# Attention of the first token chunk: from the q,k,v stage to the stage of the gates

## The chip, the cores and the metric

One Trainium2 chip with 8 cores. The kernel runs on all 8, each core on one sequence of the batch (4096 tokens of 1024 channels), with no exchange between them. The metric is the device time in microseconds (us) of the slowest core, median of the runs. A core has five engines that run side by side, each in its own program order: TensorE (PE) for matmuls, VectorE (DVE), ScalarE (ACT), GpSimd (POOL) and SyncE (SP), which here issues most DMAs.

## What is computed

One decoder layer: an attention mixer and a recurrent mixer in parallel, merged by gates, then a squared-ReLU MLP. Cut to what matters here:

```python
h = rmsnorm(x, norm1_w[l])
z = h @ w_in[l]
q, k, v, xr, yr, ga, gr = jnp.split(z, split_points, axis=-1)
...
o_attn = moba_attention(qh, kh, vh, rel_bias)     # 256-blocks: own causal block + top 3 past blocks
...
hr = rg_lru(causal_depthwise_conv(xr, ...), ...)
o_rnn = hr * jax.nn.gelu(yr)
g_attn = jax.nn.sigmoid(ga + b_gate[l, 0])
g_rnn = jax.nn.sigmoid(gr + b_gate[l, 1])
merged = g_attn * (o_attn @ w_proj_attn[l]) + g_rnn * (o_rnn @ w_proj_rnn[l])
x = x + merged @ w_out[l]
h2 = rmsnorm(x, norm2_w[l])
x = x + jnp.square(jax.nn.relu(h2 @ w_ff1[l])) @ w_ff2[l]
```

A query looks at its own block and at most three past blocks, so the first chunk of 512 tokens (blocks 0 and 1), and the second (blocks 2 and 3) leave no past block out.

## The kernel before

The sequence is cut into 32 token tiles of 128 (`NT`) and 8 chunks of 512 (`NCH`). The program is written as a list of operations with what each reads and writes; a planner (`Prog.schedule`) with a cost for each kind of operation then sets the order on every engine, greedily by readiness, and `keep_busy` puts matmuls on a tile of ones (`fill`, tile `onesf`, 128x512, the only matmuls recorded under line L1412) wherever its plan shows TensorE idle for over 0.7 us. They write nothing that is read. All other operations are recorded under L530, DMAs under L535, so rows are told apart by tile names.

Three stages follow one another on TensorE.

*q,k,v stage* (0 to about 262 us): for each token tile the norm and transposes (`FEn`), q and k with their norm (`FEp`), v (`FEv`). From tile 10 on, units of `attention0()` stand among them: attention of chunk 0 from tiles that never leave the chip (`qc0`, `kc0`, `vc0`), one unit per head and key tile: a score matmul on 64 rows ("S"), the bias on DVE, exp on ACT into `PTa`, and up to four 65-column matmuls with v ("AV"). The bias table `BT` is made for that at tiles 5 to 9, by way of a gather (`hk2`) on the POOL queue. The result goes to DRAM (`oT_s`).

*Stage of the gates* (to about 829 us), `stageB(s, g)`: x and y projections and the recurrence of chunk s (`RNN`, `RNN2`), the attention gate of chunk s (`GA`, weights `wga`), and the recurrence gate and projection of chunk s-1 (`GR`, weights `wgr`, `wpr`). For chunk 0, `GA` also multiplies by `P_attn` (weights `wps`) and `GR` adds both halves, so that the merged `mT` of chunk 0 goes to DRAM (`mT_s`). Other chunks store the two halves apart (`t1_s`, `rm_s`).

*Attention and MLP* (to the end): two lists are merged. The dense list holds the last eight units of `GR`, then for each chunk W1, W2, W1 of the second half with `gating(c+1)` between (loads of the two halves into `t1r`, `rmr`, matmul with `wpa`), `outproj(c+1)` and W2. The attention list holds `attention(c)` for c from 1. `outproj(0)` stands ahead of both lists, on the `mT` loaded by `early()`. In `attention(c)` a unit's S matmul has 64 rows for c = 1 and 80 for c > 1: the 16 more carry the block mask (`qT` rows 64 to 79, written by `GM`, against the block pattern `cE_d`). S uses two PSUM banks, and three after the last `GR`.

SP, ACT, DVE and PE wait in order: an instruction whose operand isn't ready holds all behind it on its engine, an issue on SP too.

Of the kernel before, what the change touches and what calls it, by code (L numbers as in the profile page):

```python
# [20 lines left out]
NEG = -30000.0  # L21
# [389 lines left out]
def build_nc():  # L411
# [37 lines left out]
    oT_s = scr("oT_s", [128, 4, CH], BF16)  # L449
    mT_s = scr("mT_s", [128, 8, CH], BF16)  # L450
# [28 lines left out]
    with root:  # L479
# [95 lines left out]
        wrow = alloc("wrow", [384], F32)
        Js = alloc("Js", [128], BF16)
        hk2 = alloc("hk2", [NH, 256], BF16)
        endA0 = cur[0]
        st.pop().close()
        cur[0] = endX  # L580
# [3 lines left out]
        assert endA0 <= endR  # L584
# [18 lines left out]
        qst = [alloc("qstr%d" % i, [4, 256], BF16) for i in range(2)]  # L603
        kst = [alloc("kstr%d" % i, [4, 256], BF16) for i in range(2)]
        vst = alloc("vst", [NH, VW], BF16)
# [5 lines left out]
        hT = [alloc("hT%d" % i, [8, 128], BF16) for i in range(NHT)]  # L611
        pA_peak = cur[0]
# [22 lines left out]
        for v_, vk in ((vc0, "vc0"), (vst, "vst")):  # L635
            op("gpsimd", "memset", [], [vk], ap=v_.rearrange("p a b -> p (a b)"), constant=1.0)

        def bias_table(late):
            op("vector", "memset", [], ["tabx"], ap=tabx[32:33, :], constant=NEG)
            dma("sync", tabx[0:32, :], relb_d, "c1a", [], ["tabx"], extra=late)  # L640
            dma("sync", Gs[0:33, :], cG_d, "c1b", [], ["Gs"], extra=late)
            dma("sync", Js, cJ_d, "c1c", [], ["Js"], extra=late)

        def bias_table1():
            b = tbank()
            op("tensor", "matmul", ["tabx", "Gs"], ["B%d" % b], out=bankf[b][0:8, 0:384], lhsT=tabx[0:33, :], rhs=Gs[0:33, :], start=True, stop=True)
            op("vector", "tensor_copy", ["B%d" % b], ["wrow"], out=wrow[0:8, :], in_=bankf[b][0:8, 0:384])
            dma("sync", scr_w, wrow[0:8, :], "c2", ["wrow"], ["scr_w"])
            dma("gpsimd", hk2, bass.AP(scr_w.tensor, 0, [[1, 128], [384, NH], [1, 256]]), "c3", ["scr_w"], ["hk2"])

        def bias_table2(g):
            b = rbank()
            op("tensor", "matmul", ["hk2", "Js"], ["B%d" % b], out=bankf[b], lhsT=Js, rhs=hk2[:, 2 * g:2 * g + 2, :].rearrange("p a b -> p (a b)"), start=True, stop=True)
            op("vector", "tensor_copy", ["B%d" % b], ["BT"], out=BT[:, 2 * g:2 * g + 2, :], in_=bankf[b].rearrange("p (a b) -> p a b", a=2, b=256))
# [45 lines left out]
        def FEv(t):  # L700
            c, tl = t // TPC, t % TPC
            v_, vk = (vc0, "vc0") if c == 0 else (vst, "vst")
            b = FEmm(t, 2)
            op("scalar", "copy", ["B%d" % b], [vk], out=v_[:, :, 0:260].rearrange("p h (t e) -> p h t e", t=4)[:, :, tl, 0:64],
               in_=bankf[b].rearrange("p (a b) -> p a b", a=8, b=64))
            if tl == TPC - 1:
                dma("sync", v_s[:, c], v_, vk, [vk], ["v_s%d" % c])

        def FEp(t, j):
# [20 lines left out]
            if c == 0:  # L730
                qk_, kk_, o_ = "qc0:%d" % t, "kc0:%d" % t, t * 128
                q_, k_ = qc0, kc0
            else:
                qk_, kk_ = "qstr%d" % g, "kstr%d" % g
                q_, k_ = qst[g], kst[g]
            if j == 0:
                op("vector", "tensor_copy", ["B%d" % b], [qk_], out=q_[:, :, o_:o_ + 128], in_=src)
                if t % 2 == 1 and c > 0:
                    dma("sync", q_s[c, nb_ % 2], q_, qk_, [qk_], ["q_s%d_%d" % (c, nb_ % 2)])
                return  # L740
            op("scalar", "activation", ["B%d" % b, "qkw"], [kk_], out=k_[:, :, o_:o_ + 128], in_=src, func=AF.Identity, scale=qkw)
# [737 lines left out]
```

How the kernel before makes its waits and increments, by code:

```python
        def run(ename, h):  # L335
            for i in order[ename]:
                for s, v in waits[i]:
                    h.wait_ge(sems[s], v)
                ins = ops[i].fn(h)
                if sig[i] is not None:
                    ins.then_inc(sems[sig[i][0]], 16 if ops[i].dsem is not None else 1)
            if ename == "sync":
                for s, v in fw.items():
                    h.wait_ge(sems[s], v)
```

## Time and profile before

| | |
|---|---|
| median of 3 runs | 2318.37 us (2316.98 to 2527.23) |
| the profiled execution | 2318.37 us, span of its slowest core 2316.8 us |
| other cores | 2306.9 to 2316.8 us |
| busy: PE, ACT, DVE, POOL | 2270.7, 1325.2, 1166.7, 621.5 us |
| fills on ones | 126 in the program |

The profiled execution has the median's time; 1.6 us lie outside the span. A row of the order in time gives the start, the duration and the instructions merged. Matmuls overlap, and their ends are modelled, so what one costs is read from the starts of neighbours, not from its duration. "idle before" in brackets is the wait, and what ended it.

### The profile page before, as it was taken

To read this page: it belongs to the slowest core of one execution; us is meant where nothing else is said; L and a number is where in the kernel's file an instruction comes from. 1 tells how busy PE (TensorE), PEld (TensorE's weight loads), DVE (VectorE), ACT (ScalarE), POOL (GpSimd) and SP (SyncE) were. 2 spreads that over 40 slices of the span, in tenths; PEclk is the share of its full clock that TensorE was granted. 3 is DMA by queue.
4 is the path that set the end of the run, shared out by engine and by line. 5 is a ranking of instruction groups with operands and counts; after the bars stand their busy time and mean duration, and the time that the engine had idled before them with its cause. 6 is when DMAs were issued, how large, how long until landed. Compare 5 with 4: busy or idle time off the path is not lost.

```text
span 2316.8 us, 43869 instructions; the slowest of 8 cores (2306.9 to 2316.8 us)
## 1 busy us (share of the span) xinstructions
PE 2270.7 (98%) x14604; PEld 1107.7 (48%) x14604; DVE 1166.7 (50%) x2185; ACT 1325.2 (57%) x2343; POOL 621.5 (27%) x602
## 2 busy tenths in 40 slices
PE   7999999999999999999999999999999999999999
PEld 3445444444444444454545555554555555554444
DVE  4688588787877864454253343324323422233322
ACT  4666576667676755475646646654656465562111
POOL 5776545443444430010011011102001100111200
PEclk9999999999999999999999999999999999999999
DMA  8976734676763365475455565546656554544543
GB/s 194 271 196 176 156 94 113 128 132 142 128 136 83 127 176 169 137 212 176 149 186 163 161 195 161 168 145 180 187 150 175 173 159 159 184 148 141 172 160 127
DMA packets 191559, 370.11 MB, mean 160 GB/s; under 512 B 14819, under 2 KB 105740, under 8 KB 173324
## 3 DMA queue, kind: packets, MB, share of 16 engines
q1 hardware_dynamic: 183532, 331.65, 45.9%
q0 software_dynamic: 7808, 35.65, 11.7%
q8 instruction: 124, 2.03, 0.4%
q14 instruction: 95, 0.78, 0.1%
HBM read 331.32 MB, written 90.71 MB: 182 GB/s over the span
## 4 chain that ended last, share of the span: by engine, by line
PE 89%; DMA 4%; issue 3%; DVE 2%; ACT 1%; POOL 1%; SPq 1%; DVEq 0%; ACTq 0%; POOLq 0%
PE bank L530 89%; DMA s_t1r<-t_s 1%; DMA s_nw<-nw_bc 1%; DMA s_hk<-scr_w 1%; POOL s_ssq L530 1%; SPq L535 1%; DMA s_wga<-wr_p 0%; DMA t_s<-s_t 0%; DMA s_qT<-s_mskT 0%; DVE s_cv L530 0%; DMA s_Vr<-v_s 0%; PE bank L1412 0%; ACT s_junk L530 0%; DVE s_ii L530 0%; DVE s_t1r L530 0%
## 5 line engine op out<-in xcount | busy, mean ns | idle before, releaser
L530 ACT ACTIVATE s_PT<-bank 128x512 bf16<-128x512 f32 (+1 forms) x1120 | 578.7, 566 | 319.1 <-PE bank L530 226.8
L530 PE MATMUL bank<-s_h2T,s_wsl 128*128 128x512 bf16 x2048 | 523.3, 379 | 0.0
L530 PE MATMUL bank<-s_uT,s_wsl 128*128 128x512 bf16 x2048 | 511.3, 379 | 0.0
L530 PEld LDWEIGHTS bank<-s_Vr,s_PT 128*128 128x128 bf16 x4144 | 262.9, 97 | 244.0 <-issue 12.8
L530 PE MATMUL bank<-s_qT,s_kTr 80*128 80x512 bf16 (+2 forms) x1120 | 361.6, 364 | 2.3 <-DMA s_qT<-s_mskT 2.3
L530 ACT ACTIVATE s_rl<-bank 128x512 f32<-128x512 f32 x256 | 152.7, 597 | 266.3 <-PE bank L530 254.9
L530 PE MATMUL bank<-s_Vr,s_PT 128*128 128x65 bf16 x4144 | 299.5, 193 | 3.9 <-ACT s_PT L530 2.3
L530 PEld LDWEIGHTS bank<-s_h2T,s_wsl 128*128 128x128 bf16 x2048 | 189.3, 98 | 180.5 <-issue 7.6
L530 PEld LDWEIGHTS bank<-s_uT,s_wsl 128*128 128x128 bf16 x2048 | 185.1, 98 | 171.5 <-issue 3.9
L530 POOL TENSOR_TENSOR s_uT<-s_rl 128x512 bf16<-128x512 f32 x80 | 83.8, 1048 | 620.1 <-ACT s_rl L530 617.6
L530 DVE TENSOR_TENSOR s_uT<-s_rl 128x512 bf16<-128x512 f32 x176 | 123.5, 702 | 248.1 <-ACT s_rl L530 247.7
L530 DVE TENSOR_TENSOR s_x1T<-bank,s_x1T 128x512 f32<-128x512 f32 x128 | 88.3, 690 | 315.8 <-PE bank L530 315.5
L530 DVE TENSOR_TENSOR bank<-bank,s_BT 128x256 f32<-128x256 f32 (+1 forms) x312 | 111.8, 377 | 161.7 <-PE bank L530 160.1
L530 PE MATMUL bank<-s_wqkv,s_hT 128*128 128x512 bf16 x768 | 184.5, 381 | 0.4 <-ACT s_hT L530 0.2
L530 DVE SCALAR_TENSOR_TENSOR s_cv<-s_xr,s_pvec,s_cv 128x512 f32<-128x512 f32 x192 | 163.4, 917 | 1.4 <-issue 0.6
L530 POOL TENSOR_TENSOR s_orn<-s_ii,s_gq 128x512 bf16<-128x512 f32 x64 | 115.7, 1820 | 116.5 <-DVE s_ii L530 116.4
L530 POOL TENSOR_TENSOR s_ss<-s_ss,s_sqt 128x512 f32<-128x512 f32 x48 | 60.9, 1269 | 284.9 <-ACT s_sqt L530 283.8
L530 PE MATMUL bank<-s_mT,s_wo 128*128 128x512 bf16 x512 | 132.9, 379 | 4.2 <-DVE s_mT L530 2.7
L530 POOL TENSOR_TENSOR s_mT<-s_t1r,s_rmr 128x512 bf16<-128x512 f32 x28 | 36.8, 1315 | 352.3 <-DVE s_t1r L530 250.8
L530 PEld LDWEIGHTS bank<-s_qT,s_kTr 80*128 80x128 bf16 (+1 forms) x1120 | 104.3, 98 | 50.2 <-issue 10.4
L530 PE MATMUL bank<-s_hTb,s_wga 128*128 128x512 bf16 x512 | 123.1, 383 | 3.1 <-DMA s_wga<-wr_p 3.1
L530 ACT ACTIVATE s_t<-bank,s_hbias 128x512 f32<-128x512 f32 x128 | 82.8, 680 | 71.1 <-PE bank L530 68.6
(137 smaller groups left out, 2854.5 us busy)
## 6 DMA issues: line engine op xcount, KB each, us to landing
s_wsl<-wff_s SPq DMA_DIRECT2D x128, 1024.0 KB, 5.8
s_xs<-x SPq DMA_DIRECT2D x32, 512.0 KB, 8.4
t_s<-s_t SPq DMA_DIRECT2D x64, 256.0 KB, 6.8
wff_s<-wff_p POOLq DMA_DIRECT2D x16, 1024.0 KB, 16.2
s_x1T<-xT SPq DMA_DIRECT2D x64, 256.0 KB, 3.8
outT<-s_x1T SPq DMA_DIRECT2D x64, 256.0 KB, 5.6
s_t1r<-t_s SPq DMA_DIRECT2D x56, 256.0 KB, 4.0
rm_s<-s_t SPq DMA_DIRECT2D x56, 256.0 KB, 5.7
```

The costliest lines, as they stand in the source:

```text
L530: return P.add(eng, lambda e, m=meth, kw=kw: getattr(e, m)(**kw), reads, writes, cost=c_, lat=lat, fam=fam, tag=tag or (writes[0] if write ...
L535: return P.add(q, lambda e: e.dma_start(out=out, in_=in_), reads, writes, dsem=dsem, cost=(1000.0 if q == "gpsimd" else 80.0), nbytes=nb, ...
```

## The change

`attention0()`, the merge of chunk 0 within `GA` and `GR` and the DRAM copies `oT_s`, `mT_s` are gone. Chunk 0 is now treated as the others: its q, k, v go to DRAM by `qst`, `kst`, `vst`; `attention(0)` runs in the last stage, ahead of `attention(1)`; then come `gating(0)` and `outproj(0)` at the end of the first dense stretch, ahead of W1 of chunk 0. Its S matmuls, and those of chunk 1, have 80 rows, with mask. The bias table is made later: its first matmul at tile 14, the gather behind the gate weights on the POOL queue, the rest in `stageB(2, 0)`. SBUF addresses of the last two stages are laid out anew; `wga`, `wgr`, `wpr` now alternate, panel by panel. Of what the words of the change name, the matmuls on constants (`keep_busy`) and the order of the `wqkv` loads are in both kernels alike.

```diff
-            if t == 9:
-                for g in range(4):
-                    bias_table2(g)
-                at0 = attention0()
-            if t >= 10:
-                for _ in range(2 if t < 24 else 4):
-                    if at0:
-                        at0.pop(0)()
...
-            if c == 0:
-                b = bank()
-                for kt in range(4):
-                    op("tensor", "matmul", ["oTb", "wps%d" % (p % 2)], ["B%d" % b], tag="pa", ...
...
-                op("tensor", "matmul", ["orn%d" % sos[kt], "wpr%d" % p], ["B%d" % b], tag="pr", ...
+                op("tensor", "matmul", ["orn%d" % i for i in sos] + ["wpr%d" % p], ["B%d" % b], tag="pr", ...
...
-            if c == 0:
-                dma("sync", t1x[s], t1_s[0, m], "t1x%d" % s, ["t1_s0_%d" % m], ["t1x%d" % s])
-                op("gpsimd", "tensor_tensor", ["t2_%d" % s, "t1x%d" % s], ["mst%d" % s], ...
...
-            if b >= 4:
+            if b >= 3:
...
-                        qk = ["qT%d:%d0" % (s, h % 2), "qT%d:%d1" % (s, h % 2)]
-                        kr = 64
-                        if c > 1:
-                            qk += ["qT%d:m%d" % (s, h), "kTr%d:E" % ks]
-                            kr = 80
...
+                           lhsT=kTr[ks][0:80, ...], rhs=qT[s][0:80, h, q0:CH], start=True, stop=True)
...
         def early():
+            dma("sync", wpa, wpo[:, 0:4, :], "wpa", ["wpo_s0"], ["wpa"])
             for i in range(2):
-                dma("sync", mT[:, 4 * i:4 * i + 4, :], mT_s[:, 4 * i:4 * i + 4, :], ...
                 dma("sync", wo[:, 4 * i:4 * i + 4, :], wpo[:, 4 + 4 * i:8 + 4 * i, :], ...
+            for _, f in at0[0:5]:
+                f()
+            first.append(kv0(0, 0))
 
         stageB(NCH - 1, 1, early)
-        for _, f in outproj(0):
-            f()
-        at1.pop(0)[1]()
-        first.append(kv1(1, 0))
...
+        g0 = gating(0)
         for m in range(8):
             extend([(3460.0, gate1u(m))])
+            if m == 5:
+                marks[0] = len(dense)
+            if m > 5:
+                extend(g0[2 * m - 12:2 * m - 10])
+        extend(g0[4:5])
+        for i in range(3):
+            dense.append((0.0, WLOAD))
+            extend(g0[5 + i:6 + i])
+        extend(outproj(0))
+        dense.append((6000.0, lambda: None))
```

The order that the planner makes of it. First PE where the q,k,v stage meets the gates (numbers are buffers; `cvb` against `wbda`, `wbdi` belongs to the recurrence), before:

```order
L530 MATMUL bank4<-s_cvb0,s_wbda 128x512
L530 MATMUL bank5<-s_cvb0,s_wbdi 128x512
L530 MATMUL bank1<-s_oTb,s_wps0 128x512 x4
L530 MATMUL bank6<-s_cvb1,s_wbda 128x512
L1412 MATMUL bank0<-s_onesf 128x512 x2
L530 MATMUL bank7<-s_identb,s_ktm1 128x128 x4
L530 MATMUL bank3<-s_oTb,s_wps0 128x512 x4
L1412 MATMUL bank0<-s_onesf 128x512 x6
L530 MATMUL bank0<-s_hTb0,s_wga0 128x512 x8
```

and now PE in the same place, from the first matmul with `wga`:

```order
L528 MATMUL bank2<-s_hTb0,s_wga1 128x512 x4
L528 MATMUL bank7<-s_identb,s_ktm1 128x128 x4
L528 MATMUL bank3<-s_cvb0,s_wbdi 128x512
L528 MATMUL bank2<-s_hTb0,s_wga1 128x512 x4
L528 MATMUL bank4<-s_hTb0,s_wx2 128x512 x3
L528 MATMUL bank7<-s_cvb2,s_wbdi 128x512
L528 MATMUL bank4<-s_hTb0,s_wx2 128x512 x2
L528 MATMUL bank3<-s_hTb0,s_wga1 128x512 x8
L528 MATMUL bank4<-s_hTb0,s_wx2 128x512 x3
L528 MATMUL bank5<-s_hTb0,s_wy2 128x512 x5
L528 MATMUL bank0<-s_hTb0,s_wga0 128x512 x8
```

Panel 1 of `wga` comes ahead of panel 0, projections stand between, and the fills are gone. Next PE behind the last gate matmuls of the stage of the gates (`qT,kTr` are S, `Vr,PT` AV, `mT,wo` is `outproj`), before:

```order
L530 MATMUL bank<-s_hTb,s_wgr 128x512 x4
L530 MATMUL bank<-s_mT,s_wo 128x512 x32
L530 MATMUL bank<-s_hTb,s_wgr 128x512 x4
L1412 MATMUL bank<-s_onesf 128x512 x9
L530 MATMUL bank<-s_hTb,s_wgr 128x512 x8
L1412 MATMUL bank<-s_onesf 128x512 x9
L530 MATMUL bank<-s_mT,s_wo 128x512 x32
L530 MATMUL bank<-s_orn,s_wpr 128x512 x8
```

and now, in the same place:

```order
L528 MATMUL bank<-s_qT,s_kTr 128x384
L528 MATMUL bank<-s_qT,s_kTr 128x512
L528 MATMUL bank<-s_hTb,s_wgr 128x512 x14
L1318 MATMUL bank<-s_onesf 128x512 x9
L528 MATMUL bank<-s_hTb,s_wgr 128x512 x16
L1318 MATMUL bank<-s_onesf 128x512 x14
L528 MATMUL bank<-s_orn,s_wpr 128x512 x5
L528 MATMUL bank<-s_Vr,s_PT 128x65 x4
L528 MATMUL bank<-s_qT,s_kTr 128x256
```

The 64 `outproj` matmuls no longer stand there; 96 fills in 25 places lie between the last gates of this stage and W1, where there were 20 in 3. Last SP in the same place (`rm_s` are the stores of `GR`), before:

```order
L535 DMA s_qT<-q_s 64x4x256 x4
L535 DMA s_Vr<-v_s 128x2x288 x4
L535 DMA rm_s<-s_t_0 128x512
L535 DMA rm_s<-s_t_1 128x512
L535 DMA rm_s<-s_t_0 128x512
```

and now SP there, from the last store of chunk 6:

```order
L533 DMA rm_s<-s_t_1 128x512
L533 DMA s_qp<-q_s 128x4x256 x2
L533 DMA s_Vr<-v_s 128x2x288 x4
L533 DMA s_qT<-q_s 64x4x256 x4
L533 DMA s_kTr<-c_E 16x4096
L533 DMA s_kTr<-k_s 64x4x256 x4
L533 DMA s_t1r<-t_s 128x512
L533 DMA rm_s<-s_t_0 128x512
L533 DMA rm_s<-s_t_1 128x512
```

Fifteen loads of chunk 1 and one of `gating(0)` stand ahead of the next stores of `GR`; further on, `gating(0)` adds eight pairs of loads.

## Rows read from the trace of the kernel before

**Rows 1.** The page, busy time of TensorE.
```profile
PE 2270.7 (98%) x14604; PEld 1107.7 (48%) x14604; DVE 1166.7 (50%) x2185; ACT 1325.2 (57%) x2343; POOL 621.5 (27%) x602
```

**Rows 2.** The page, chain that ended last, by engine.
```profile
PE 89%; DMA 4%; issue 3%; DVE 2%; ACT 1%; POOL 1%; SPq 1%; DVEq 0%; ACTq 0%; POOLq 0%
```

**Rows 3.** Windows: length, busy PE, PEld, DVE, ACT, POOL; then granted clock, DMA share, GB/s.
```profile
36.00:128.00 92.00, 86.07 (x543) 43.54 (x544) 64.77 (x104) 58.44 (x97) 68.36 (x88) 1.00 0.92 245
128.00:262.00 134.00, 132.60 (x866) 68.56 (x865) 105.72 (x197) 86.09 (x153) 89.09 (x109) 1.00 0.63 171
262.00:275.00 13.00, 8.30 (x45) 3.71 (x44) 4.81 (x9) 7.67 (x11) 7.23 (x10) 1.00 0.98 187
275.00:280.00 5.00, 5.00 (x17) 1.92 (x16) 0.69 (x1) 0.69 (x1) 3.31 (x4) 0.66 1.04 190
280.00:345.00 65.00, 62.68 (x288) 27.55 (x286) 55.87 (x79) 49.01 (x76) 31.30 (x25) 1.00 0.44 105
829.00:885.00 56.00, 52.65 (x260) 23.14 (x258) 30.84 (x49) 24.41 (x38) 15.53 (x11) 1.00 0.54 141
```

**Rows 4.** PE in order of time, chunk 1, S of 64 rows.
```profile
859.36 0.28 PE L530 MATMUL bank<-s_Vr,s_PT 128*128 128x65 bf16 x4 [1.24 <-DMA s_Vr<-v_s]
859.58 0.39 PE L530 MATMUL bank<-s_qT,s_kTr 64*128 64x512 bf16 x1
859.89 0.39 PE L530 MATMUL bank<-s_orn,s_wpr 128*128 128x512 bf16 x1
```

**Rows 5.** PE in order of time, a later chunk, S of 80 rows.
```profile
1117.62 0.28 PE L530 MATMUL bank<-s_Vr,s_PT 128*128 128x65 bf16 x4
1117.74 0.38 PE L530 MATMUL bank<-s_qT,s_kTr 80*128 80x512 bf16 x1
1117.96 1.68 PE L530 MATMUL bank<-s_h2T,s_wsl 128*128 128x512 bf16 x7
```

**Rows 6.** PE in order of time, first fills behind 36 us.
```profile
92.63 1.67 PE L1412 MATMUL bank<-s_onesf 128*128 128x512 bf16 x7
```

**Rows 7.** PE in order of time, where the stage of the gates begins.
```profile
274.72 5.30 PE L530 MATMUL bank<-s_hTb,s_wga 128*128 128x512 bf16 x16 [3.07 <-DMA s_wga<-wr_p]
...
282.66 3.62 PE L530 MATMUL bank<-s_hTb,s_wga 128*128 128x512 bf16 x16
```

**Rows 8.** PE in order of time, from that stage's end to W1.
```profile
837.82 2.11 PE L1412 MATMUL bank<-s_onesf 128*128 128x512 bf16 x9
840.25 1.89 PE L530 MATMUL bank<-s_hTb,s_wgr 128*128 128x512 bf16 x8 [0.32 <-ACT s_t L530]
841.97 2.11 PE L1412 MATMUL bank<-s_onesf 128*128 128x512 bf16 x9
845.55 7.07 PE L530 MATMUL bank<-s_mT,s_wo 128*128 128x512 bf16 x32 [1.48 <-DVE s_x1T L530]
...
888.23 0.59 PE L1412 MATMUL bank<-s_onesf 128*128 128x512 bf16 x2
888.66 2.75 PE L530 MATMUL bank<-s_h2T,s_wsl 128*128 128x512 bf16 x12
```

**Rows 9.** POOL in order of time, last results of the recurrence.
```profile
843.41 3.34 POOL L530 TENSOR_TENSOR s_orn<-s_ii,s_gq 128x512 bf16<-128x512 f32 x2 [3.09 <-DVE s_ii L530]
```

**Rows 10.** SP in order of time, the same place.
```profile
850.08 2.53 SPq L535 DMA_DIRECT2D s_qT<-q_s  x4
...
856.69 16.59 SPq L535 DMA_DIRECT2D rm_s<-s_t  x5
```

**Rows 11.** DMA issues: KB each, median us to landing.
```profile
s_t1r<-t_s SPq DMA_DIRECT2D x56, 256.0 KB, 4.0
```

**Rows 12.** Chain in order of time, a wait for such a load.
```profile
1192.74 8.46 DMA s_t1r<-t_s
```

**Rows 13.** Groups by shape: busy, mean ns of one, idle before.
```profile
L530 DVE SCALAR_TENSOR_TENSOR s_t1r<-s_t1r,bank 128x512 f32<-128x512 f32 x56 | 38.3, 684 | 36.1 <-PE bank L530 25.4 <-DMA s_t1r<-t_s 10.1
L530 POOL TENSOR_TENSOR s_mT<-s_t1r,s_rmr 128x512 bf16<-128x512 f32 x28 | 36.8, 1315 | 352.3 <-DVE s_t1r L530 250.8 <-DVE bank L530 47.5 <-DVE s_rcp L530 46.0
```

More of the change, by code:

```diff
@@ L634, in build_nc @@
         op("vector", "memset", [], ["hstate"], ap=hstate, constant=0.0)
[L635 to L636 removed]
+        for i in range(1):
+            op("gpsimd", "memset", [], ["vst%d" % i], ap=vst[i].rearrange("p a b -> p (a b)"), constant=1.0)
         def bias_table(late):
[L639 to L642, printed above, removed]
+            op("vector", "memset", [], ["ii0"], ap=tabx[32:33, :], constant=NEG)
+            dma("sync", tabx[0:32, :], relb_d, "c1a", [], ["ii0"], extra=late)
+            dma("sync", Gs[0:33, :], cG_d, "c1b", [], ["cv0"], extra=late)
@@ L651, in bias_table2 @@
[L651 to L654, printed above, removed]
+            op("tensor", "matmul", ["ii0", "cv0"], ["B7"], out=bankf[7][0:8, 0:384], lhsT=tabx[0:33, :], rhs=Gs[0:33, :], start=True, stop=True)
@@ new lines, in bias_table1, with bias_table2, bias_table3 @@
+            op("vector", "tensor_copy", ["B7"], ["rr0"], out=wrow[0:8, :], in_=bankf[7][0:8, 0:384])
+            dma("sync", scr_w, wrow[0:8, :], "c2", ["rr0"], ["scr_w"])
+        def bias_table2():
+            dma("sync", Js, cJ_d, "c1c", [], ["Js"])
+            dma("gpsimd", hk2, bass.AP(scr_w.tensor, 0, [[1, 128], [384, NH], [1, 256]]), "c3", ["scr_w"], ["hk2"])
+        def bias_table3():
+            for g in range(4):
+                b = dbank()
+                op("tensor", "matmul", ["hk2", "Js"], ["B%d" % b], out=bankf[b], lhsT=Js, rhs=hk2[:, 2 * g:2 * g + 2, :].rearrange("p a b -> p (a b)"), start=True, stop=True)
+                op("vector", "tensor_copy", ["B%d" % b], ["BT"], out=BT[:, 2 * g:2 * g + 2, :], in_=bankf[b].rearrange("p (a b) -> p a b", a=2, b=256))
@@ L1059, in build_nc @@
[L1059 to L1068 removed]
+        t1r = [alloc("t1r0", [CH], F32)]
@@ new lines, in build_nc @@
+        assert cur[0] <= endR, (cur[0], endR)
+        if endR - cur[0] > 64:
+            alloc("gap2", [(endR - cur[0]) // 64 * 32], BF16)
+        mT = alloc("mT", [8, CH], BF16)
+        oT.append(alloc("oT1", [4, CH], BF16))
+        NRL = 2
+        rl = [alloc("rl%d" % i, [CH], F32) for i in range(NRL)]
+        t1r.append(alloc("t1r1", [CH], F32))
+        rmr = [alloc("rmr%d" % i, [CH], F32) for i in range(2)]
+        assert cur[0] <= baseC, (cur[0], baseC)
+        uT = alloc("uT", [16, CH], BF16)
@@ L1069, in build_nc @@
+        NW = 4
+        wsl = [alloc("wsl%d" % i, [4096], BF16) for i in range(NW)]
+        NX1 = 12
+        x1T = alloc("x1T", [NX1, CH], F32)
+        h2T = alloc("h2T", [8, CH], BF16)
         p2_peak = cur[0]
@@ L1207, in attention @@
             units.append((0.0, lambda: QLOAD(c)))
-            if c > 1:
-                units += [(100.0, lambda tl=tl: GM(c, tl)) for tl in range(TPC)]
+            units += [(100.0, lambda tl=tl: GM(c, tl)) for tl in range(TPC)]
             for h in range(NH):
@@ L1233, in WLOAD @@
             s = i % NW
-            dma("sync", wsl[s], wff_s[i % 16], "wsl%d" % s, ["wff_s%d" % (i % 16)], ["wsl%d" % s])
+            dma("sync", wsl[s], wff_s[i % 16], "wsl%d" % s, ["wff_s%d" % (i % 16)], ["wsl%d" % s], extra=P.after("mT:%d" % i) if i < 3 else ())
         def gating(c):
@@ L1387, in build_nc @@
                 extend(w2)
-        queue = [(u[0], u[1], 1) for u in at1]
-        for c in range(2, NCH):
-            for u in attention(c):
+        queue = [(u[0], u[1], 0) for u in at0[5:]]
+        tot0 = sum(q_[0] for q_ in queue)
+        for c in range(1, NCH):
+            us = attention(c)
+            if c == 1:
+                queue[16:16] = [(u[0], u[1], 0) for u in us[:5]]
+                us = us[5:]
+            for u in us:
                 queue.append((u[0], u[1], c))
```

223 lines of the change are left out of this document (59 added, 164 removed).

## Prediction

> **What bounds the kernel now.** I read the page first. TensorE is busy 98% of the span [rows 1], and the chain that ended last lies on it for 89% [rows 2]: what counts is the matmul time in program order, and the places where TensorE waits. No other engine comes near. So every part of the change is priced on TensorE: work that vanishes or appears there, fills that do, and pauses.
>
> A busy share hides what a matmul costs, since a matmul's row overlaps the next one's. The order in time gives the cost, from start to start. Eight 512-column matmuls take 841.97 - 840.25 = 1.72 us [rows 8], so 0.215 us for one, a fill too. Then I looked for pauses by stage, as length minus busy time [rows 3]: 5.9 us from 36 to 128, 1.4 to 262, 4.7 in the 13 us where the gates begin, 2.3 from 280 to 345, and 3.4 from 829 to 885, where the last stage begins.
>
> **The change part by part.** The attention of chunk 0, its gating matmuls (32 with `wpa` for 32 with `wps`) and its output projection exist on both sides. Moved work that meets a TensorE without idle time costs the same there. What is left is six terms.
>
> *Scores on 80 rows instead of 64: -17.7 us.* In chunk 1 an AV of four takes 859.58 - 859.36 = 0.22 us and the S behind it 859.89 - 859.58 = 0.31 [rows 4]. In a later chunk, with 80 rows, they take 0.12 and 0.22 [rows 5]. The columns are the same, so each stretch of 64-row matmuls costs 0.19 us more, about half going in and half coming out. Chunk 0 and chunk 1 have 96 such S, which stand in 93 separate stretches of the order; 93 x 0.19 = 17.7. All of them stand beside dense matmuls, so TensorE pays it today, and no cover is lost with it. The Trainium skill speaks on both sides here. "TensorE: Matmul & The Clock Gate", section "Why this matters for your kernels", has a single matmul on few rows take as long as one on 128, which leaves nothing to save, and the sum would be 17.7 us higher. "TensorEngine Tiling (Array Packing)", section "Key Properties", says that changing the tiling mode drains the engine, which would be this term, without a price. The two rows agree with the second.
>
> *Fills that go from the first two stages: -5.4 us.* From 36 to 345 us there were 27 in 7 places (the first: [rows 6]); 2 are left. 25 x 0.215 = 5.4. Fills run whether or not TensorE would have waited, so this is sure.
>
> *Pauses in the first two stages: -6 us, between -2 and -11.* They are 14.3 us from 36 to 345 [rows 3]. The wait of 3.07 us for the first `wga` panel [rows 7] should go, and what else TensorE waits in those 13 us, 4.7 in all: the loads of `wps` ahead of the panel are gone, and the order puts `wga1` ahead of `wga0`, with projections between. The rest comes from norms and recurrence, which stay. The bias gather moves behind the gate weights on POOL, and nobody waits for it until the third chunk.
>
> *The clock behind that wait: -1.7 us.* The 16 `wga` matmuls after it take 5.30 us, the same 16 later 3.62 [rows 7], and the granted clock from 275 to 280 is 0.66 [rows 3], so partly the lower of its two levels, after a stretch of waits. If the wait goes, so do these 1.7 us.
>
> *Fills in the last stage: +17.4 us.* Between the end of the gates and W1 there are 96 instead of 20, and behind that 23 instead of 18: 81 x 0.215 = 17.4, as sure as the fills above. They mark where the planner found nothing to do. Before, `outproj(0)` filled the time until the recurrence of chunk 7 is done: its last results land at 843.41 + 3.34 = 846.75 [rows 9], 17.7 us after the last gate groups of that stage at 829. Now only 32 gate matmuls (6.9 us) and two S (0.4) can run there, so some 10.4 us are open, 23 fills (4.9 us) among them. After that the attention of chunk 0 is paced by S, bias, exp, AV on two score banks; the gate matmuls run out before its heads do.
>
> *Pauses that the fills don't cover: +15 us, between -2 and +39.* Behind the two groups of nine, which themselves take 1.94 us, 0.49 and 1.64 us were lost [rows 8]; behind the group of two at 888.23 the next starts 0.43 later, so nothing. The mean of three is 0.7; 25 places give 17.5, less the 2.1 of today, which is 15. The lower end is no pause at all, the upper one 1.64 at each place. I take the mean, since the nearest rows are in the same stage; the 5.5 us still open above are part of it.
>
> *Loads on SP: +7 us, between 0 and +21.* One issue of a q load takes 2.53 / 4 = 0.63 us [rows 10]. The 15 loads of chunk 1 ahead of the stores of `GR` hold SP for some 9 us, and with it the two buffers `t2` and the banks behind them. Today 18 issues stand there too, and the stores come at 856.69 [rows 10], but `outproj(0)` covers it; now the heads of chunk 0 do, in part: I take 4, between 0 and 9. Further on, `gating(0)` has two buffers for eight pairs of loads, so three rounds follow the first, each a load, a DVE product of 0.68 and a POOL sum of 1.3 us [rows 13]. At the median landing of 4.0 us [rows 11] with 0.3 of issue a round is 6.3 us and three are 19; beside them TensorE has the 64 units of chunk 1, where a full unit is 0.34 us [rows 5], so at most 22 us, in fact about 18 since a quarter of them are cut, and some 14 fills, 3 us. That just covers it. At 8.46 us, as in the chain later [rows 12], three rounds are 32, and 12 stick out. I take 3. What queues behind on SP are the loads of x for `outproj(0)` and of the W1 slabs; TensorE waits for both.
>
> *Small:* 16 more mask and gate matmuls, each shorter than a fill; under 1 us, I take 0.7.
>
> The sum: -17.7 - 5.4 - 6 - 1.7 + 17.4 + 15 + 7 + 0.7 = +9.3 us, on the profiled execution's 2318.37, which is also the median: 2328 us. With all favourable ends it is -17.7 - 5.4 - 11 - 1.7 + 17.4 - 2 + 0 + 0.7 = -19.7, so 2299; with all unfavourable ones -17.7 - 5.4 - 2 - 0 + 17.4 + 39 + 21 + 0.7 = +53, so 2371.
>
> **The rivals.** *The chain of chunk 0 becomes the path (slower).* Place: attention 0, `gating(0)`, `outproj(0)`, norm, W1, one behind the other, beside whatever GR and chunk 1 still have. It decides from a landing of `t1r` of about 4.7 us, where three rounds outlast the 21 us beside them; at 8.46 us and with 1.64 us lost in front of each of the 25 places, the result is the upper end, 2371. For it: TensorE's order is fixed, so one late load holds all behind it, and the sixteen loads of `gating(0)` come one round after the other. Against it: the planner that set the order knew these dependencies, and before, its pauses came out small [rows 8].
>
> *The waits don't appear (slightly faster).* The fills run, but behind them the operands are there: no pauses and no stall on SP, 2318.4 - 30.8 + 17.4 - 2 + 0.7 = 2304. For it: the third group of today lost nothing. Against it: the 10.4 us behind the recurrence are open whatever the fills do [rows 9].
>
> *The 64 rows were not the cause.* If the extra 0.19 us came with the place and not with the rows, or if a single short matmul costs as much as a full one (the rule in "TensorE: Matmul & The Clock Gate" above), the first term falls away: 2346. The two pairs of rows speak against it.
>
> That the change doesn't do what its words say holds in part: fills and the order of the `wqkv` loads are in both kernels. It has no time of its own, since the sum uses only what differs.
>
> **How the numbers follow.** My forecast, a small loss from terms that nearly cancel, gets 0.62; the slower rival 0.16, the faster one 0.15, the 64 rows 0.05; 0.02 are left for a gain that I don't see. A measurement of this kernel can tell about 2%, 46 us, from no change. The forecast, the faster rival and the third lie within that. The slower rival ends above 2365, and most of its chance counts as slower, some more from the forecast's tail: 0.17. Faster by over 2% needs 46 us, while all savings together are 36: 0.03. The range, 2302 to 2366, leaves about 0.15 above and 0.05 below.
>
> **What would show it.** All S have 80 rows, AV takes 0.12 and S 0.22 in chunks 0 and 1 too. The first two stages end some 30 us sooner (attention and `wps` out of them, and the terms above), around 798; W1 begins around 912, where it was 885, and from there the stages run alike, shorter by what chunk 1 had left. No wait for `wga0`, and a clock of 1.00 there. Between the gates and W1 some 96 fills and 15 to 25 us of pauses. Wrong I would be if the pauses there were over 40 us, if a wait of several us dropped the clock there as at 275, or if the later stages, which I take as unchanged, waited on loads that now come in another order.

## The result and the profile after

The changed kernel takes 2379.84 us (median of 4 runs, 2372.06 to 2384.7), the kernel before 2317.74 beside it: a ratio of 1.0266, interval 1.0225 to 1.0307. It is slower by some 62 us; 9 were forecast, with 2366 as the upper end of the range. Some executions of all these kernels were disturbed, and the ratios compare the others, so the text goes by ratios; in us they are the ratio times 2318.4.

The page of the profile after first, with the lines that answer to [rows 1, 2]; the line PEclk gives the granted clock in 40 slices of the span:

```profile
span 2374.1 us, 44166 instructions; the slowest of 8 cores (2339.4 to 2374.1 us)
PE 2292.8 (97%) x14676; PEld 1116.1 (47%) x14676; DVE 1170.3 (49%) x2225; ACT 1328.0 (56%) x2343; POOL 613.8 (26%) x593
PE   7999789999999988999999999999999999999999
PEclk9999999999999997999999999999999999999999
PE 83%; DMA 5%; issue 4%; DVE 3%; POOL 3%; ACT 1%; SPq 1%; DVEq 0%; POOLq 0%; ACTq 0%
```

A busy share of 97% instead of 98% looks harmless. The slices say where to look: the fifth and the sixth (237 to 356 us), and the 15th and 16th (831 to 950 us), in the second of which the clock drops too. The chain lies on PE for 83% instead of 89% [rows 2].

The same in windows of the changed kernel (length, PE busy, number of instructions, granted clock, DMA share, GB/s), to set against [rows 3]:

```profile
36.00:128.00 92.00, 85.95 (x544) 1.00 0.85 248
...
262.00:275.00 13.00, 6.12 (x29) 0.93 0.69 146
275.00:280.00 5.00, 0.62 (x2) 0.50 0.61 107
...
400.00:450.00 50.00, 44.51 (x200) 0.97 0.60 114
...
825.00:912.00 87.00, 75.57 (x468) 0.96 0.54 154
912.00:945.00 33.00, 28.02 (x182) 0.60 0.86 253
945.00:965.00 20.00, 18.15 (x104) 0.98 0.07 19
```

Where the gates begin, 11 of 18 us are empty. Just before W1 TensorE is busy, but at a granted clock of 0.60, so for most of it on the lower of its two levels. Apart from a load at the very start (14.97 us), the three longest transfers on the chain, in order of time, stand at these places:

```profile
251.04 22.25 DMA q_s<-s_qst
...
429.42 17.36 DMA rm_s<-s_t
...
907.43 13.96 DMA s_t1r<-t_s
```

All three carry 256 KB; the load that I took from [rows 11] lands in 4.0 us. The first was the dearest. POOL in order of time (in brackets: idle before, and what ended it):

```profile
254.04 0.53 POOL L533 DMA_DIRECT2D s_wgr<-wr_p  x1 [0.41 <-PE bank L528]
257.34 1.03 POOL L528 TENSOR_TENSOR s_rr<-s_aa 128x512 f32<-128x512 f32 x1 [2.78 <-DVE s_aa L528]
273.88 0.57 POOL L533 DMA_DIRECT2D s_wpr<-wpr_p  x1 [15.51 <-DMA q_s<-s_qst]
274.48 2.04 POOL L528 TENSOR_TENSOR s_rr<-s_aa 128x512 f32<-128x512 f32 x2
```

and PE:

```profile
267.09 1.03 PE L528 MATMUL bank<-s_hTb,s_wy 128*128 128x512 bf16 x4
279.38 0.59 PE L528 MATMUL bank<-s_cvb,s_wbda 128*128 128x512 bf16 x1 [11.27 <-ACT s_t L528]
```

and ACT, which stands between the two:

```profile
275.62 0.63 ACT L528 ACTIVATE s_rr<-s_rr 128x512 f32<-128x512 f32 x1 [14.57 <-POOL s_rr L528]
...
278.55 1.27 ACT L528 ACTIVATE s_t<-bank,s_hbias 128x512 f32<-128x512 f32 x2
```

The fourth `wpr` panel takes the place in SBUF where the last q tile is staged, so its load, on POOL, waits for that tile's store. Behind it in POOL's queue stand the squares of the recurrence (`rr`). ScalarE waits 14.57 us for these, its `s_t` behind them frees no bank, and TensorE stands still for 11.27 us. Who was in the store's way is seen in the DMA issues from 240 to 262 us (queue 0 is POOL's, queue 1 SP's; packets, MB, share of the engines; then KB and us to landing):

```profile
q0 software_dynamic: 1133, 2.19, 69.3%
q1 hardware_dynamic: 1065, 2.27, 34.2%
...
s_hTb<-h_s SPq DMA_DIRECT2D x1, 1024.0 KB, 21.3
s_wga<-wr_p POOLq DMA_DIRECT2D x2, 512.0 KB, 13.5
s_wgr<-wr_p POOLq DMA_DIRECT2D x2, 512.0 KB, 19.3
v_s<-s_vst SPq DMA_DIRECT2D x1, 576.0 KB, 23.0
...
q_s<-s_qst SPq DMA_DIRECT2D x1, 256.0 KB, 22.2
```

On its own queue the store follows a load of 1 MB and a store of 576 KB, and POOL's gate panels take as many bytes as that whole queue. On core 1 the load of `hTb` lands in 7.1 us (issued at 241.70; until 248.8 SP's queue moves 1.23 MB and POOL's 0.18), the q store in 9.8, and TensorE loses 3.2 us there, not 11. Cores 1, 3 and 7 are of this kind, the five others of the first.

For all cores, medians over the eight of each run, from the first and last matmul of the groups with `wga`, `h2T` (W1) and `uT` (W2); the range is that of the cores:

| kernel | last wga, us | from there to W1 | W1 to the last W2 |
|---|---|---|---|
| before | 822.9 (819.6 to 828.3) | 59.8 | 1423.6 |
| after | 818.6 (803.4 to 824.7) | 135.0 | 1400.0 |
| forecast, as a change | -31 | +58 | -18 |
| measured, as a change | -4 | +75 | -24 |

The profiled core of after, 4, is the worst: last `wga` at 824.7, then 140.7 us, then 1404.0. Against the profiled core of before (825.5, 60.0, 1427.0) that is -0.8, +80.7 and -23.0, together the 57 us between the spans.

### The profile page after: what moved, and what is told of

It reads as the page before. It is cut to its first block, busy times and chain, and to the rows that moved or that the text cites. A ratio compares the mean times of both kernels' runs of the same rounds, so it can differ in the third digit from the quotient of the medians.

```text
span 2374.1 us, 44166 instructions; the slowest of 8 cores (2339.4 to 2374.1 us)
## 1 busy us (share of the span) xinstructions
PE 2292.8 (97%) x14676; PEld 1116.1 (47%) x14676; DVE 1170.3 (49%) x2225; ACT 1328.0 (56%) x2343; POOL 613.8 (26%) x593
## 4 chain that ended last, share of the span: by engine, by line
PE 83%; DMA 5%; issue 4%; DVE 3%; POOL 3%; ACT 1%; SPq 1%; DVEq 0%; POOLq 0%; ACTq 0%
PE bank L528 82%; POOL s_ssq L528 2%; DMA s_t1r<-t_s 1%; DMA q_s<-s_qst 1%; SPq L533 1%; DMA rm_s<-s_t 1%; DMA s_nw<-nw_bc 1%; DVE s_cv L528 1%; DMA outT<-s_x1T 1%; PE bank L1318 1%; DVE s_ii L528 0%; DMA s_qT<-s_mskT 0%; DVE s_ssq L528 0%; DMA s_x1T<-xT 0%; DVE s_t1r L528 0%
## 5 line engine op out<-in xcount | busy, mean ns | idle before, releaser
L528 ACT ACTIVATE s_PT<-bank 128x512 bf16<-128x512 f32 (+3 forms) x1152 | 590.1, 563 | 314.0 <-PE bank L528 192.1
L528 PE MATMUL bank<-s_uT,s_wsl 128*128 128x512 bf16 x2048 | 518.9, 379 | 1.7 <-DVE s_x1T L528 1.0
L528 PE MATMUL bank<-s_h2T,s_wsl 128*128 128x512 bf16 x2048 | 516.8, 380 | 0.8 <-DVE s_h2T L528 0.8
L528 PEld LDWEIGHTS bank<-s_Vr,s_PT 128*128 128x128 bf16 x4224 | 272.8, 98 | 262.7 <-issue 26.6
L528 PE MATMUL bank<-s_qT,s_kTr 80*128 80x512 bf16 (+3 forms) x1152 | 373.0, 367 | 6.3 <-DMA s_qT<-s_mskT 3.1
L528 PE MATMUL bank<-s_Vr,s_PT 128*128 128x65 bf16 x4224 | 314.1, 194 | 5.5 <-ACT s_PT L528 4.8
L528 PEld LDWEIGHTS bank<-s_qT,s_kTr 80*128 80x128 bf16 x1152 | 108.3, 99 | 51.1 <-issue 12.6
L528 PE MATMUL bank<-s_orn,s_wpr 128*128 128x512 bf16 x512 | 124.6, 385 | 5.0 <-POOL s_orn L528 5.0
```

The source lines that it names most:

```text
L528: return P.add(eng, lambda e, m=meth, kw=kw: getattr(e, m)(**kw), reads, writes, cost=c_, lat=lat, fam=fam, tag=tag or (writes[0] if write ...
```

## Experiments

**The theory.** Transfers of 256 KB that share the DMA engines with loads of 0.5 and 1 MB come 10 to 20 us late. TensorE's order is fixed, so what waits for them (a queue, two buffers, a matmul) holds all the rest, and behind such waits the clock falls. **The rival.** No transfer is to blame: the loss is the 17 us of fills and the pace of the last stage (attention 0, one gating round behind the other), which the prediction's slower rival has. Two terms of the prediction, the rows and the fills, are tested beside them.

The measured places of all runs, as in the table above. The median core is the median of the eight spans, as a mean over the executions that the ratio compares (of before, ten from the runs beside late_panels, before_no_fills and before_rows128):

| kernel | ratio to before, interval | median core, us | last wga | to W1 | W1 to end |
|---|---|---|---|---|---|
| before | | 2312.2 | 822.9 | 59.8 | 1423.6 |
| after | 1.0266, 1.0225 to 1.0307 | 2359.1 | 818.6 | 135.0 | 1400.0 |
| late_wpr3 | 1.0175, 1.0155 to 1.0195 | 2354.4 | 811.3 | 139.2 | 1398.3 |
| late_panels | 1.0197, 1.0172 to 1.0221 | 2355.4 | 815.0 | 136.1 | 1399.9 |
| late_slabs | 1.0172, 1.0123 to 1.0222 | 2347.4 | 819.6 | 126.0 | 1402.6 |
| both_late | 1.0136, 1.0121 to 1.0150 | 2342.4 | 809.0 | 126.1 | 1403.9 |
| all_late | 1.0156, 1.0140 to 1.0171 | 2347.1 | 811.2 | 129.0 | 1403.2 |
| no_fills | 1.0273, 1.0178 to 1.0367 | 2370.1 | 826.8 | 142.8 | 1401.9 |
| more_fills | 1.0223, 1.0202 to 1.0245 | 2362.6 | 821.8 | 141.5 | 1396.5 |
| rows_64 | 1.0296, 1.0253 to 1.0339 | 2375.6 | 821.3 | 148.0 | 1401.2 |
| before_no_fills | 1.0024, 1.0014 to 1.0033 | 2317.0 | 826.2 | 60.4 | 1427.2 |
| before_rows80 | 0.9950, 0.9932 to 0.9968 | 2298.2 | 824.7 | 58.3 | 1411.2 |
| before_rows128 | 0.9929, 0.9910 to 0.9948 | 2296.0 | 821.3 | 58.4 | 1411.7 |

The time is the slowest core's, and which cores meet the long store changes from run to run; the median core and the column "to W1" are steadier. From before to after the median core loses 47 us, the slowest 62: the 15 between are that lottery.

**The load behind the store, moved.**

```diff
-            dma("gpsimd", wpr[p], ...)
+            if p < 3:
+                dma("gpsimd", wpr[p], ...)
...
+                if (s, g) == (0, 1):
+                    dma("gpsimd", wpr[3], ..., extra=P.after("orn3"))
```

> The changed kernel with one load moved: the fourth wpr panel is issued on POOL after the first four recurrences of chunk 0, not between the first and the second square of their gates. In the changed kernel that load waits on POOL 15.5 us for the store of the last q tile, which took 22.3 us beside five gate panels of 512 KB each, and TensorE loses 11.3 us behind it. Transfer theory (short transfers that share the DMA engines with bulk loads come 10 to 17 us late, and a queue or a buffer hands that on to TensorE): that wait is gone on all cores that have it, the last wga matmul comes at some 805 to 812 us instead of 818 to 825, and the time falls by 8 to 13 us, to 2367 to 2372. Pace theory (the loss is fills and attention work that the last stage's chain paces; the store is no cause): the wait comes back at the next step of the recurrence, and the time stays at 2376 to 2384.

Measured: 1.0175, 2359 us, 21 us less than after, more than expected. No core has the wait: idle time of TensorE from 252 to 345 us is 8.1 to 10.6 us on all eight, where it was 19.6 to 22.1 on five cores and 9.2 to 10.2 on three. The last `wga` of core 4:

```profile
L528 PE MATMUL bank<-s_hTb,s_wga x512: 376/379/631, 252.5 to 812.1; 128*128 128x512 bf16 x171
```

12.6 us sooner than in after (824.7). The store itself stays slow (21.2 us on that core, 19 to 23 on six of the eight); only nobody waits for it. Most of the gain is the slowest core's: it stood 19 us above the median core in the profiled execution of after and stands 4 above it here. The median core gains 5, since the stretch to W1 has grown from 135.0 to 139.2 us; what takes these 4 us back was not tried.

**The traffic before the store, moved.**

```diff
-  ... "wga%d" % p, [], ["wga%d" % p])
+  ... "wga%d" % p, [], ["wga%d" % p], extra=P.after("q_s7_1") if p == 3 else ())
-  ... "wgr%d" % p, [], ["wgr%d" % p])
+  ... "wgr%d" % p, [], ["wgr%d" % p], extra=P.after("q_s7_1") if p in (0, 3) else ())
```

> The changed kernel in which three gate panels (wga3, wgr0, wgr3) are issued once the store of the last q tile has landed; the fourth wpr panel still waits on POOL for that store, with three gate squares behind it. What changes is the traffic that the store meets: two panels instead of five. Transfer theory: the store lands in 5 to 11 us on all cores instead of 20 to 23 on five of them, POOL's wait shrinks to under 5 us, TensorE's wait of 10 to 12 us there to under 4, the last wga matmul comes at 802 to 814 us, and the time is 2360 to 2372. If the 22 us are the store's own (many small pieces, HBM), not the panels' traffic: store, waits and time stay, 2376 to 2384.

Measured: 1.0197, 2364 us. The wait stays in POOL's queue, but it is short. On core 4 the 1 MB load ahead of the store lands in 7.1 us instead of 21.3. DMA issues and POOL in order of time there:

```profile
s_hTb<-h_s SPq DMA_DIRECT2D x1, 1024.0 KB, 7.1
```

```profile
264.39 0.63 POOL L533 DMA_DIRECT2D s_wga<-wr_p  x1 [2.21 <-DMA q_s<-s_qst]
```

On all eight cores the q stores land in 7.9 to 11.6 us (three of these are medians of two stores) and POOL waits 2.2 to 6.1; TensorE's longest wait there is 2.7. The 1 MB load still takes 14.8 to 16.8 us on four of the cores, so the store need not wait for it to land early. The last `wga` comes at 808 to 820 us, somewhat later than expected. So the 22 us were the panels' traffic, not the store's own. This and the run before settle the first place.

**The slabs, moved.**

```diff
-        for i in range(3):
-            dense.append((0.0, WLOAD))
-            extend(g0[5 + i:6 + i])
+        extend(g0[5:8])
+        for i in range(3):
+            dense.append((0.0, WLOAD))
...
-  extra=P.after("mT:%d" % i) if i < 3 else ())
+  extra=P.after("mT:7") if i < 3 else ())
```

> The changed kernel with the first three weight slabs (1 MB each) loaded after the last mT of chunk 0 instead of after the first, second and third. In the changed kernel the load of the third t1r takes 13.96 us behind two slabs and eight x loads, TensorE loses 0.9 and 2.0 us there, and the granted clock is 0.61 from 912 to 940 us. Transfer theory: the t1r loads land in 4 to 8 us, the clock stays near 1.00 in that stretch or falls for less time, W1 begins 8 to 18 us sooner, and the time falls to 2362 to 2372. Pace theory: the units of chunk 1 are paced by bias and exp whatever the loads do; W1 begins within 4 us of before and the time is 2374 to 2384. If the slabs now come too late for W1, the time is up to 2392 and TensorE waits for the slab at the start of W1.

Measured: 1.0172, 2358 us; from the gates to W1 126.0 us instead of 135.0. The late load on the chain of core 4, and the stretch in which the clock was 0.60:

```profile
902.01 8.29 DMA s_t1r<-t_s
```

```profile
912.00:945.00 33.00, 30.71 (x207) 0.87 0.55 175
```

8.29 us instead of 13.96, and a clock of 0.87; from 800 us to W1 it is 0.93 to 0.98 on the eight cores, where it was 0.90 to 0.95. The time came out a little better than expected, the median core gains 12 us, and on core 4 the mechanism is the theory's. On other cores the longest `t1r` load on the chain goes either way (core 6: 11.72 us in after, 5.23 here; core 1: 8.08 and 10.97), so for them it isn't shown. The edit also changed the planner's order: 88 instead of 96 scores stand ahead of W1, some 2.7 us at 0.34 a unit [rows 5], and W1 to the end is 2.6 us longer. So by the places about 6 of the 9 us are gained, and the rest is moved.

**Both moves.** Both edits together.

> The changed kernel with both moves together: the fourth wpr panel behind the first recurrences, the three slabs behind the last mT of chunk 0. Alone they gave 2360 and 2362, after 2380. Transfer theory: they act at different places, so they add up: the last wga at some 810 us, W1 some 125 us later, 2338 to 2348. If one only uncovers what the other hides, the time is 2352 to 2362.

Measured: 1.0136, 2350 us, just above the expected 2338 to 2348. On the median core they do add up, 5 and 12 to 17 us, and by place: last `wga` at 809, then 126.1 us. The order of late_slabs is in it, with 88 scores ahead of W1. What does not add up is the slowest core's part, which each move alone had gained in some measure.

**The x loads, moved too.**

```diff
-  ... "xl%d" % xi, [], [xk], extra=P.after("mT:%d" % (dt_ // 2)) if c == 0 else ())
+  ... "xl%d" % xi, [], [xk], extra=P.after("mT:%d" % (4 + dt_ // 2)) if c == 0 else mt7[0] if c == 1 and dt_ < 4 else ())
```

> The same, and the loads of x for the output projection too: those of chunk 0 behind the fifth to the eighth mT instead of the first to the fourth, and the four of chunk 1 that were issued with them behind the last. With the slabs moved, the slowest t1r load still takes 8.3 us behind twelve x loads of 256 KB. Transfer theory: t1r lands in 4 to 5 us, W1 begins 4 to 10 us sooner than with the two moves alone, the time is 2330 to 2340. Pace theory (what is left is attention 0 and the gating rounds themselves): W1 begins within 3 us of there. If x now comes too late for the projection: 3 to 8 us slower than there.

Measured: 1.0156, 2355 us: the third case, x too late. Core 4, DMA issues from 880 to 935 us:

```profile
s_x1T<-xT SPq DMA_DIRECT2D x12, 256.0 KB, 13.5
...
s_t1r<-t_s SPq DMA_DIRECT2D x8, 256.0 KB, 4.0
```

`t1r` lands in 4.0 us, as in the kernel before, and the output projection begins 94 to 98 us after the last `wga` (98 to 103 with the two moves alone). But now x has the long landing, and from the projection to W1 it takes 32 to 35 us instead of 25 to 27. The bytes seem to have to come in that stretch anyway, so that the order only picks who is late.

**Fills, none and more.** In after, 0 and 180 in place of 96 between gates and W1:

```diff
-            if t - a > self.WGAP - 200.0:
+            if t - a > self.WGAP - 200.0 and not 700e3 < t < 950e3:
```

```diff
-                m = int((t - a) * 0.8 / 216.0)
+                m = int((t - a) * (1.4 if 700e3 < t < 950e3 else 0.8) / 216.0)
```

> The changed kernel without the 96 fills between the end of the gates and W1; the 86 others stay. At 0.215 us each they are 20.7 us of TensorE. Pace theory, and the prediction's term 'fills in the last stage, as sure as the fills above': the time falls by their length where TensorE had work, so by 12 to 21 us, to 2359 to 2368. Transfer theory: they stand where the operands are late anyway, so TensorE waits as long without them, W1 begins within 5 us of where it did, and the time is 2374 to 2384; if the granted clock then falls earlier, it is slower, up to 2400.

> The changed kernel with 180 fills instead of 96 between the end of the gates and W1: 84 more, 18.1 us of TensorE. Without any, TensorE's idle time there was 34 to 37 us instead of 18 to 20, the granted clock 0.80 to 0.83 instead of 0.90 to 0.95, and W1 began some 6 us later relative to the last gate. If fills only take the place of waits and hold the clock up: the clock there is 0.95 or more and W1 begins 0 to 8 us sooner, 2372 to 2382. If they cost what they last once they reach past the waits: 6 to 18 us slower, 2386 to 2398, at a clock that is also higher.

Measured: 142.8 us without and 141.5 with 180, against 135.0 with 96. Taking 20.7 us of matmuls away made this stretch 8 us longer, and 18.1 us more made it 6 longer. Idle time of TensorE from 800 us to W1 was 33 to 38 us without, 17 to 20 with 96, 11 to 18 with 180; the clock over that stretch 0.80 to 0.83, 0.90 to 0.95, 0.95 to 0.98. With the fills at 0.215 us each, the time without real work is 33 to 38, 37 to 41 and 50 to 56 us. So TensorE has some 35 to 40 us without work here, which 96 fills still fit into; most of the 84 more reach past the waits and cost time. What the stretch loses without fills goes with the lower clock, as the time without work hardly changed. The ratios of the two decide nothing by themselves, the one for its wide interval, the other since it depends on how many cores met the long store. The median core agrees in sign, 11 us slower without fills and 3 slower with 180, but the 11 are a mean of two executions that lie 14 apart, and in the profiled one the last `wga`, ahead of all that was changed, came 8 us late.

> The kernel before without its 65 fills behind the start (27 up to 345 us, 20 in the last stage's beginning, 18 later); the 61 at the start stay. At 0.215 us they are 14.0 us. If fills cost what they last, as two terms of the prediction have it: 2303 to 2307, a ratio of 0.994 to 0.996. If TensorE waits in their place: 2315 to 2322, within 0.2% of before, with 10 to 14 us more idle time on TensorE; if the clock then falls in one of these places, up to 2328.

The same in the kernel before, all 65 fills behind the start:

```diff
-            if t - a > self.WGAP - 200.0:
+            if t - a > self.WGAP - 200.0 and t < 40e3:
```

Measured: 1.0024, interval 1.0014 to 1.0033: 14.0 us of matmuls less, and 5.6 us more. In the stage of [rows 8], on core 2 of that run:

```profile
829.00:885.00 56.00, 49.44 (x223) 0.94 0.55 141
```

The same core of before has 53.71 us busy there at a clock of 1.00; the difference is the 20 fills (4.3 us). The waits came back in the fills' place, and the clock fell somewhat.

**The rows.** In after the scores of chunks 0 and 1 on 64 rows; in the kernel before those of chunk 1 on 80, and then those of chunk 0 on 128 with zeros.

```diff
+            kr = 64 if c < 2 else 80
...
-  lhsT=kTr[ks][0:80, ...], rhs=qT[s][0:80, h, q0:CH]
+  lhsT=kTr[ks][0:kr, ...], rhs=qT[s][0:kr, h, q0:CH]
```

```diff
-            if egeo[s] != g and c > 1:
+            if egeo[s] != g:
-                        if c > 1:
+                        if c > 0:
-            if c > 1:
+            if c > 0:
                 units += [(100.0, lambda tl=tl: GM(c, tl)) for tl in range(TPC)]
```

```diff
-        qc0 = alloc("qc0", [4, CH], BF16)
+        qc0 = alloc("qc0", [NH, CH], BF16)
...
-  lhsT=kc0[r0:r0 + 64, hp, q0:q0 + 128], rhs=qc0[r0:r0 + 64, hp, q0:CH]
+  lhsT=kc0[:, hp, q0:q0 + 128], rhs=qc0[:, h, q0:CH]
```

> The changed kernel with the scores of chunks 0 and 1 on 64 rows again (the mask rows are loaded but not used; for these two chunks they change nothing). The prediction's term has 93 stretches at 0.19 us each, 17.7 us, all paid. Transfer theory: part of these scores now stand where TensorE waits for operands anyway, so less is paid: 5 to 14 us, 2384 to 2395. If the term is right as it stands: 2395 to 2400. If the rows were not the cause: 2378 to 2382.

Measured: the median core is 16.5 us slower, and the stretch to W1 148.0 us instead of 135.0. The ratio, 1.0296, is only 7 us above after's, with intervals that overlap. I had expected that 4 us and more of the 17.7 hide in waits; idle time of TensorE from 800 us to W1 does fall, to 12 to 14 us from 17 to 20, but by the median core nearly as much is lost. The clock over that stretch is 0.87 to 0.88 here, against 0.90 to 0.95, so a part of the 16.5 is the clock's; how much is the rows' own in this kernel stays open.

> The kernel before, with the scores of chunk 1 on 80 rows, for which it gets the mask units and mask loads that later chunks have; chunk 0 stays as it is. The prediction's first term, applied to the 64 scores of chunk 1: some 62 stretches at 0.19 us, 11.8 us less, and under 1 us for the mask; TensorE has next to no idle time there (3.4 us in 56), so all of it should show: 2306 to 2309, a ratio of 0.995 to 0.997. If the rows are not the cause, or the eight mask loads on SP delay the stores behind them: 2316 to 2324.

Measured: 0.9950, 11.6 us less (7 to 16 by the interval, some 14 on the median core), where 11.8 had been worked out; W1 to the end is 12.4 us shorter.

> The kernel before with the scores of chunk 1 on 80 rows, and those of chunk 0, in the q,k,v stage, on 128: each head's q stands beside rows of zeros where the other head's k is. It costs one more copy for each of the first four tiles (on ScalarE) and a zeroing of 8 KB a partition. The prediction's term for the 32 scores of chunk 0: 32 x 0.19 = 6.1 us less than with chunk 1 alone (2310, a ratio of 0.995), so 2303 to 2306, 0.992 to 0.9935. If the dense stage hides the switch, or the copies at the start delay it: 2308 to 2313.

Measured: 0.9929, 16.5 us less than before, 2302 us. The further 4.9 us would fit the 6.1, but the intervals of the two overlap, and the median core gains only 2.2 of them; so for chunk 0 the size stays open between 2 and 6. PE in order of time in the q,k,v stage:

```profile
201.39 0.27 PE L530 MATMUL bank<-s_identb,s_qa 128*128 128x128 bf16 x2
201.50 0.27 PE L530 MATMUL bank<-s_qc,s_kc 128*128 128x256 bf16 x1
201.61 1.89 PE L530 MATMUL bank<-s_wqkv,s_hT 128*128 128x512 bf16 x8
```

The same three steps in the kernel before, on 64 rows:

```profile
202.28 0.27 PE L530 MATMUL bank<-s_identb,s_qa 128*128 128x128 bf16 x2
202.49 0.28 PE L530 MATMUL bank<-s_qc,s_kc 64*128 64x256 bf16 x1
202.70 1.90 PE L530 MATMUL bank<-s_wqkv,s_hT 128*128 128x512 bf16 x8
```

0.22 us from the first start to the third instead of 0.42. This kernel is faster than the kernels before and after.

## Why the prediction was wrong

**Scores on 80 rows, -17.7: right.** Put into the kernel before, where TensorE hardly waits, the edit is worth 11.6 us for chunk 1 (11.8 by the prediction's price) and 16.5 for both chunks. In the changed kernel taking the rows back cost the median core 16.5 us, the clock's part included; the rows' own sign is there as predicted, 0.12 us for an AV and 0.22 for an S (core 4):

```profile
895.03 0.29 PE L528 MATMUL bank<-s_Vr,s_PT 128*128 128x65 bf16 x4
895.15 0.38 PE L528 MATMUL bank<-s_qT,s_kTr 80*128 80x512 bf16 x1
895.37 0.38 PE L528 MATMUL bank<-s_oT,s_wpa 128*128 128x512 bf16 x1
```

"TensorEngine Tiling (Array Packing)" of the Trainium skill, section "Key Properties", says that a change of tiling mode drains the engine; the runs agree, at 0.2 us for one short matmul among full ones.

**Fills, -5.4 in the first two stages and +17.4 in the last: wrong, both.** "Fills run whether or not TensorE would have waited" is true of the instructions and false of the time. Without its fills the kernel before is 5.6 us slower, and without the 96 the transition of the changed one is 8 us longer, at a lower clock. A fill that fits into a wait costs nothing here (84 more, most of which did not fit, cost 6 us); what counts is the time without work, fills and pauses together. Counted so, the prediction had it at 8.7 us from 36 to 345 (14.3 of pauses [rows 3] and 5.8 of fills, less 5.4 and 6) and at some 46 from the gates to W1 (7.7 today, 16.3 for 76 more fills, 15 and 7). On the profiled core it was 31.6 (31.4 and one fill) and 39.3 (18.7 and 20.6). The sum in the last stage was about right, for a wrong reason; the first two stages carried the error.

**Pauses in the first two stages, -6: this step failed first.** They came out at 31.4 us on the profiled core where 8.3 were forecast, and 18 on core 1, which has no long wait. The prediction saw the `wps` loads gone and took the rest as unchanged. It did not follow that the panels now share SBUF with other buffers of the stage before, that one load on POOL therefore waits for a store, and that the recurrence stands behind it in POOL's queue. The order of the changed kernel shows the wait; its price stood in no row of before and had to be bounded. With the clock behind it (0.83 from 280 to 290 us) and 2.7 us more of waits from 345 to 450 (5.5 instead of 2.8; the rm store of 17.36 us, behind two casts of 1 MB), the stages ended 30 us later than the forecast on that core. late_wpr3 and late_panels show the cause by taking away either side of it. Even without it the pauses there do not fall: on core 4 of late_wpr3 21.3 us stay from 36 to 345, as much as before's pauses and fills together (14.3 and 5.8), so the savings of -5.4 and -6 did not come at all. New pauses stand in the q,k,v stage, which attention 0 has left: from 128 to 240 us TensorE waits 4.1 to 6.0 us on the eight cores of that run (and of after), most of it for the norms of q and k, where before had 1.4 to 2.4 and 3 fills. The term took the rest of the pauses as unchanged and missed these.

**The clock behind the wga wait, -1.7: the wrong sign,** by the same wait.

**Pauses that fills don't cover, +15: right in size.** 18.7 us were measured from 829 to 966, inside the 15 to 25 that were to show it; they hold the pauses of the next term too (the longest are 3.27 us for the recurrence and 1.97 for a `t1r` product), so the two terms can't be told apart by it.

**Loads on SP, +7, up to 21: too small.** The term rested on 4.0 us for a `t1r` landing, with 8.46 as the worst. Beside three slabs and twelve x loads the median of five was 8.7 and the worst 13.96. The slower rival had 4.7 us as its turning point, so its condition held. What neither had is the clock: "if a wait of several us dropped the clock there" was on the list of what would make the prediction wrong, without a price. At 0.60 for 33 us, 28.0 us of busy time are what 17 would be at the full clock, an estimate of 11 us from that row; the 87 us before at 0.96 add some 3. late_slabs, with the clock at 0.87 in these 33 us, gave back 9 of the 135, about 6 of them for good.

**W1 at 912: 965.4.** Of the 53 us, 30 come from the first two stages and some 14 from the clock. The rest, about 10 net of the 7 by which fills and pauses stayed under their forecast, is probably attention, which no run tested: all 96 scores of chunks 0 and 1 ran ahead of W1, where 13 of chunk 1's 64 had; the forecast for the stages behind W1, -18, came out at -24 by the median core, so part of it was given back.

The forecast gave the slower rival 0.16. It ended near the right time (2371), but with one half of the loss where it looked and the other half at a place that no rival named. By the runs, 21 us go back with the load behind the store, 22 with the slabs, 30 with both (5, 12 and 17 on the median core); the 32 that stay against before are the time without work between the gates and W1, which the attention of chunk 0 filled with the projections beside it when it ran in the q,k,v stage. That last sentence is argued from the windows; no run moved the attention back alone.

## What to carry to other kernels

Count the time in which the bottleneck engine has no real work, fills and waits together: a filler that fits into a wait was free here, and those taken out saved nothing. Where buffers change places in SBUF, look for each load that now waits for a store, and for what stands behind it in its queue; price it by the traffic of that moment, not by the median landing of the whole run. A gain that shows in one operation's rows (the 0.2 us for scores on 64 rows) can be taken alone: in the old kernel it gave 16.5 us, in the new one it came with a schedule that lost some 79 (the 62 and the 16.5, if the rows are worth as much there).

## What the runs showed of the hardware

A transfer of 256 KB took from 2.4 us (the median of the `t_s` stores on core 4) to 22.2 (the q store) in the same kernel, by what was in its way. From 240 to 262 us the two queues of core 4 moved 2.27 and 2.19 MB in 1065 and 1133 packets, nearly equal shares, though POOL's packets took 69.3% of the engines' time and SP's 34.2. "DMA: Bandwidth & Descriptors" of the Trainium skill, section "Queues, rings and completion order", has each DMA engine take turns between its queues, packet by packet; the trace of these 22 us agrees with it. By that rule, with packets as equal as here, a store that has 1.6 MB ahead of it on its own queue waits for about as many bytes of the other one too.

Equal programs on eight cores met that traffic in two ways, 3.3 us apart in their arrival (the q store is issued at 247.70 on core 1 and at 251.04 on core 4): 9.8 or 22.2 us for the same store. Core 1 differs in that POOL's queue moved next to nothing (0.18 MB) in the 7.1 us of the `hTb` load. Why, and why five cores fell to one side and three to the other, stays open.

A single matmul of 64 rows among those of 128 costs 0.2 us more than one of 80 or of 128 rows with zeros in half of them.
